# Modulation groups moved beside projections and into routing in a two-network kernel, with early column-half statistics

## The reference, cut to what matters

```python
cs = jax.nn.silu(c)
for l in range(DEPTH):                                   # first network, DEPTH = 2
    mod = (cs @ ada_w[l] + ada_b[l])[:, None, :]         # ada_w[l] is 1024 x 6144
    sh1, sc1, g1, sh2, sc2, g2 = jnp.split(mod, 6, axis=-1)
    h = rms_norm(x, norm1_g[l]) * (1.0 + sc1) + sh1
    ...                                                  # y: even mixer for l = 0, odd mixer for l = 1
    x = x + g1 * y
    h = rms_norm(x, norm2_g[l]) * (1.0 + sc2) + sh2
    x = x + g2 * hier_moe(h, ...)                        # 16 experts of 256 hidden columns, routed
return rms_norm(x, final_g)
...
mod = (c_act @ w_mod[l] + b_mod[l])[:, None, :]          # second network
h = layer_norm(x) * (1.0 + sc1) + sh1
y = hybrid_mixer(...)
x = layer_norm(DEEPNORM_ALPHA * x + (1.0 + gt1) * y, ln1_g[l], ln1_b[l])
h = layer_norm(x) * (1.0 + sc2) + sh2
y = hierarchical_moe(h, ...)                             # 16 experts of 512 hidden columns
x = layer_norm(DEEPNORM_ALPHA * x + (1.0 + gt2) * y, ln2_g[l], ln2_b[l])
```

## Time and profile before

| | us |
|---|---|
| median of 3 runs | 1359.21 |
| lowest, highest | 1359.13, 1361.91 |
| the profiled execution | 1359.62 |
| its span, first to last instruction | 1357.9 |

### The profile page before, as it was taken

The page is one execution under the profiler, slowest core; times in us unless marked ns, Lnnn a source line. Parts: engine busy times, 40 slices in busy tenths (PEclk is TensorE's granted clock), DMA queues, the critical chain, the costliest instruction groups (busy, mean ns, idle before and its releaser), DMA issues.

```text
span 1357.9 us, 17790 instructions
## 1 busy us (share of the span) xinstructions
PE 1232.0 (91%) x7440; PEld 649.5 (48%) x7440; DVE 444.3 (33%) x1148; ACT 267.6 (20%) x621; POOL 115.8 (9%) x202
## 2 busy tenths in 40 slices
PE   4999987999799899799999999899999599999895
PEld 4445743435445665344448845555545343333332
DVE  1102643113203574421153642431132731201124
ACT  0102511122101354212112122002320311020010
POOL 1010010000011000100001000000000222222221
PEclk9899997999999799989999999999999799999998
DMA  9956964999983565469999533383326579999993
GB/s 355 369 177 205 368 202 141 348 373 387 384 291 124 205 233 184 139 211 348 380 386 387 210 124 124 124 300 136 114 101 216 218 253 362 382 387 387 386 385 122
DMA packets 222955, 357.43 MB, mean 263 GB/s; under 512 B 15845, under 2 KB 86038, under 8 KB 222870
## 3 DMA queue, kind: packets, MB, share of 16 engines
q1 hardware_dynamic: 209056, 352.33, 73.6%
q10 hardware_dynamic: 13814, 3.87, 1.3%
HBM read 355.14 MB, written 1.05 MB: 262 GB/s over the span
## 4 chain that ended last, share of the span: by engine, by line
PE 82%; DVE 7%; DMA 4%; ACT 3%; issue 2%; SPq 1%; POOL 0%; DVEq 0%; ACTq 0%
PE bank L2117 20%; PE bank L2318 8%; PE bank L2524 8%; PE bank L2367 4%; PE bank L2810 4%; PE bank L2210 4%; PE bank L2135 4%; DMA ring<-in_w_down 3%; PE bank L2859 3%; PE bank L2293 3%; PE bank L2596 2%; PE bank L2387 2%; PE bank L2202 2%; PE bank L2227 1%; PE bank L2475 1%
## 5 line engine op out<-in xcount | busy, mean ns | idle before, releaser
L2117 PE MATMUL bank<-ring,hT 128*128 128x512 f32 x416 | 183.8, 601 | 3.3 <-ACT hT L895 2.4
L2117 PEld LDWEIGHTS bank<-ring,hT 128*128 128x128 f32 x416 | 79.2, 193 | 99.4 <-issue 98.6
L2524 PE MATMUL bank<-ring,A 128*64 128x512 f32 x512 | 116.5, 601 | 1.8 <-DVE pb L1722 1.8
L2318 PE MATMUL bank<-ring,A 128*64 128x512 f32 x512 | 117.2, 603 | 0.0
L2135 PE MATMUL bank<-ring,cact 128*32 128x128 f32 x2304 | 82.1, 297 | 18.0 <-issue 10.4
L2117 PE MATMUL bank<-ring,OT 128*128 128x512 f32 x224 | 97.2, 593 | 1.3 <-ACT OT L1212 0.8
L751 POOL TENSOR_TENSOR rstd<-rstd,nhalf 128x1 f32<-128x1 f32 x20 | 17.2, 859 | 810.2 <-DVE rstd L1281 810.2
L2135 PEld LDWEIGHTS bank<-ring,cact 128*32 128x32 f32 x2304 | 68.3, 119 | 33.4 <-issue 25.8
L2524 PEld LDWEIGHTS bank<-ring,A 128*64 128x64 f32 x512 | 35.1, 138 | 72.2 <-issue 70.7
L2117 PEld LDWEIGHTS bank<-ring,OT 128*128 128x128 f32 x224 | 42.2, 190 | 53.5 <-issue 52.5
L2318 PEld LDWEIGHTS bank<-ring,A 128*64 128x64 f32 x512 | 34.5, 138 | 66.6 <-issue 66.6
(11 more groups left out here) (470 smaller groups left out, 1663.5 us busy)
## 6 DMA issues: line engine op xcount, KB each, us to landing
ring<-in_ada_w SPq DMA_DIRECT2D x24, 2048.0 KB, 10.1
ring<-in_moe_w_gate SPq DMA_DIRECT2D x32, 1024.0 KB, 8.0
ring<-in_moe_w_up SPq DMA_DIRECT2D x32, 1024.0 KB, 10.6
ring<-in_moe_w_down SPq DMA_DIRECT2D x16, 2048.0 KB, 19.7
ring<-in_w_gate SPq DMA_DIRECT2D x16, 2048.0 KB, 11.6
ring<-in_w_up SPq DMA_DIRECT2D x16, 2048.0 KB, 11.0
ring<-in_w_down SPq DMA_DIRECT2D x16, 2048.0 KB, 20.1
ring<-in_w_in SPq DMA_DIRECT2D x13, 2048.0 KB, 19.6
```

The source lines that it names most:

```text
L2117: ins = mm(B[2 * (m % 2) + tt][:], lhs[:, c, tt * P:(tt + 1) * P], w[:, c, :], start=c == 0, stop=c == C - 1)
L2318: ins = mm(B[r][64 * b:64 * (b + 1), :], wide_h[c][:, slot:slot + 64], w[:, 2 * r + b, :], start=c == 0, stop=c == C - 1)
L2524: ins = mm(B[r][64 * b:64 * (b + 1), :], wide_h[c][:, slot:slot + 64], w[:, 2 * r + b, :], start=c == 0, stop=c == C - 1)
```

## The change

It has four parts.

1. **Order of loads.** `PHASES` interleaves the tiles of `mod_b` with those of `evin` and the tiles of `mod_c` with those of `odin`. `mod_h2` and `mod_h4` move from behind their MoE to the place ahead of it.
2. **Summed by DVE.** For groups 1, 2, 4 and 5 DVE multiplies the eight chunks of a tile by their entries of `cact` and sums them into one 128x512 tile (`mod_sum`, eight instructions, each waiting for the one before). PE adds its 128 rows with four matmuls against ones (`mod_summed_tile`), behind a tile of the projection. The turns come behind tile 3 and at the end. The attentions hold no modulation any more and wait for it ahead of their first scores.
3. **Routing.** In MoE 0 and 1 PE computes the four tiles of groups 3 and 6 in the routing, three between the router and the places and one behind them; the turn stands behind the first gather, DVE's columns ahead of its gathers.
4. **Statistics and halves.** `added` takes the statistics of each column half when it has been added, and the overflow flag is loaded earlier. In MoE 2 the column halves run outside and the experts' halves inside, summed in the bank, so that x is added to twice instead of four times; the last norm's centred product runs ahead of the wait for its power.

The diff, cut to its core:

```diff
-PHASES = [("mod_a", 4), ("evin", 6), ("mod_b", 8), ("evout", 2), ("moe0", 24), ("mod_h2", 4),
-          ("odin", 5), ("cmp", 2), ("mod_c", 8), ("odout", 2), ("moe1", 24), ("mod_h4", 4),
+EVIN = [("evin", 0), ("mod_b", 0), ("evin", 1), ("mod_b", 1), ("mod_b", 2), ("evin", 2), ("mod_b", 3), ("evin", 3),
+        ("mod_b", 4), ("mod_b", 5), ("evin", 4), ("mod_b", 6), ("mod_b", 7), ("evin", 5)]
+ODIN = [("odin", 0), ("mod_c", 0), ("odin", 1), ("mod_c", 1), ("mod_c", 2), ("odin", 2), ("mod_c", 3), ("mod_c", 4),
+        ("odin", 3), ("mod_c", 5), ("mod_c", 6), ("odin", 4), ("mod_c", 7)]
+PHASES = [("mod_a", 4), EVIN, ("evout", 2), ("mod_h2", 4), ("moe0", 24),
+          ODIN, ("cmp", 2), ("odout", 2), ("mod_h4", 4), ("moe1", 24),
           ("xbc", 4), ("z", 2), ("qkv", 3), ("mod_gated", 4), ("ssdo", 2), ("gates", 4), ("atto", 1),
...
+SUMMED = {1: 0, 2: 4, 4: 8, 5: 12}
...
+        def mod_sum(G, k):
+
+            n, order = mod_tile_of(G, k), SUMMED[G] + k
+            acc = tmp[:, order % 2, :]
+            w = ring[n % NSLOT][:].rearrange("p (c n) -> p c n", n=512)
+            dve.wait_ge(landed[n % NSLOT], LANDED[n])
+            if order >= 2:
+                tile_ready(dve, mod_tile_of(*SUM_TILES[order - 2]))
+            step(v.tensor_scalar(acc, w[:, 0, :], cact[:, 0:1], None, ALU.mult))
+            for c in range(1, C):
+                ins = v.scalar_tensor_tensor(acc, w[:, c, :], cact[:, c:c + 1], acc, ALU.mult, ALU.add)
+                if c < C - 1:
+                    step(ins)
+            ins.then_inc(s["mod_summed"], 1)
...
-                for step in mod_chunk_steps(name, t):
-                    mod_tile(*step)
...
+        def mod_summed_tile(G, k):
+
+            if k == 0:
+                pe.wait_ge(s["mod_raw_out"], G)
+            pe.wait_ge(s["mod_summed"], SUMMED[G] + k + 1)
+            acc = tmp[:, (SUMMED[G] + k) % 2, :]
+            for q in range(4):
+                ins = mm(B[MOD_RAW_BANK[G]][32 * q:32 * (q + 1), k * P:(k + 1) * P], tri_one[:, P:P + 32],
+                         acc[:, q * P:(q + 1) * P], start=True, stop=True)
+            ins.then_inc(tile_used, 1)
...
+        def evin_mod(j):
+
+            if j == 3:
+                mod_turn(1)
+            for G, k in (((1, 0),), ((1, 1), (1, 2)), ((1, 3),), ((2, 0), (2, 1)), ((2, 2), (2, 3)), ())[j]:
+                mod_summed_tile(G, k)
+
+        project("evin", 6, hT, turned="h0", between=qk_group, after=evin_mod)
+        mod_turn(2)
         stage_transposed(pe, "qk0")
+        pe.wait_ge(s["mod_ready"], 3)
...
+            for G, k in (((4, 0),), ((4, 1), (4, 2)), ((4, 3), (5, 0)), ((5, 1), (5, 2)), ((5, 3),))[j]:
+                mod_sum(G, k)
...
+                    dve.wait_ge(s["wide_added"], past("wide_added", i) + 2 * j + tt + 1)
+                    step(v.bn_stats(stats[:, tt, j, :], xs))
+            mod_columns(MOE[name]["mod"])
...
+            G = MOE[name]["mod"]
             router(i, MOE[name]["hname"])
+            for k in range(3):
+                mod_tile(G, k)
             places(i)
+            mod_tile(G, 3)
             gather(0, 0)
+            mod_turn(G)
...
-        mod_group(3)
...
-            for half in range(2):
-                for j in range(2):
+            for j in range(2):
+                for half in range(2):
...
+        powers = [norm_begin(x, tt, LN_EPS, True, ()) for tt in range(TT)]
+        dve.wait_ge(s["rows_param"], 16 * 5)
+        for tt in range(TT):
+            step(v.scalar_tensor_tensor(x[:, tt, :], x[:, tt, :], mv[:, tt, 0:1], rowp[:, 0, :],
+                                        ALU.subtract, ALU.mult))
         for tt in range(TT):
             dve.wait_ge(s["pow_done"], powers[tt])
-            gain(tt, 5, True).then_inc(s["result"], 1)
+            v.scalar_tensor_tensor(x[:, tt, :], x[:, tt, :], rstd[:, tt:tt + 1], rowp[:, 1, :],
+                                   ALU.mult, ALU.add).then_inc(s["result"], 1)
```

More of the change, by code:

```diff
@@ L580, in columns, with mixed @@
                      w.rearrange("(c p) n -> p c n", p=P)[:, :, col0 + 512 * j:col0 + 512 * (j + 1)])
+        def mixed(phase, sources):
+            for name, j in phase:
+                w, col0 = sources[name]
+                n = TILE_NO[name, j]
+                load(n, n % NSLOT, kview(n % NSLOT),
+                     w.rearrange("(c p) n -> p c n", p=P)[:, :, col0 + 512 * j:col0 + 512 * (j + 1)])
         def moe_small(name, wg, wu, wd):
@@ L2104, in bank_pair_free, with project @@
                 proj_evacuated(pe, m - 2)
-        def project(name, tiles, lhs, first=0, turned=None, between=None):
+        def project(name, tiles, lhs, first=0, turned=None, between=None, after=None):
             for j in range(first, tiles):
@@ L2124, in project, with mod_tile @@
                         between(g)
-        def mod_tile(G, k, chunks=range(C)):
-            if k == 0 and chunks[0] == 0 and G:
+                if after is not None:
+                    after(j)
+        def mod_tile(G, k):
+            if k == 0 and G:
                 pe.wait_ge(s["mod_raw_out"], G)
@@ L2132, in mod_tile @@
             c0 = C if G >= 6 else 0
-            for c in chunks:
+            for c in range(C):
                 for q in range(4):
@@ L2732, in qkv_group, with odin_mod @@
             transposes("qkv1", from_tokens(pb), [g])
-        project("odin", 5, hT, turned="h2", between=qkv_group)
+        def odin_mod(j):
+            if j == 3:
+                mod_turn(4)
+            for G, k in (((4, 0),), ((4, 1), (4, 2)), ((4, 3), (5, 0)), ((5, 1), (5, 2)), ((5, 3),))[j]:
+                mod_summed_tile(G, k)
+        project("odin", 5, hT, turned="h2", between=qkv_group, after=odin_mod)
         m = PROJ["odin"] + 5
```

160 lines of the change are left out of this document (76 added, 84 removed).

## The result

The changed kernel takes **1394.61 us** (median, 1394.27 to 1395.01), beside 1359.24 us for the kernel before on the same chip: 1.025 of it, 95% interval 1.0235 to 1.0266. The direction is the one forecast. The size is not: +35.4 us where I had +14, and 1394.6 lies outside 1360 to 1380. Its profiled execution has a span of 1393.1 us, 35.2 more than before, and a mean granted clock of 0.944 instead of 0.965.

A forecast was written before the change was run, and what follows sets the result against it. PE, 82% of the chain, was taken to bound the kernel, in the small MoEs together with DMA's weights. Terms 3.5+0+9.2-3.3+7-2.2 = 14.2 gave 1373.8 against the profiled time, 1373.4 against the median: forecast 1373, range 1360 to 1380.

The forecast's parts named there:

- Attention 0 and 1: Both attentions: shorter with the modulation taken out, by 1.0 us in attention 0 and 3.3 us in attention 1.
- The argument about DVE's chain: Attention 0: DVE's chain of 2.4 us stands as before, so an item takes 4.19 us instead of 4.35.
- Rival D: Both attentions lose their clock without modulation, about 4 us each, 8 in both: 1381; chance 0.10.
- Odd projection: Odd projection: 4.0 us for eight summed tiles, turns and switches, and 5.3 of PE wait for DVE's copy: +9.2.
- B: Odd projection: no PE wait, which takes sums of 3.5 us: 1368; chance 0.12.
- C: Odd projection: sums and ropes hold each other, the wait growing by a rope's 2.3 us: 1376; chance 0.12.
- Even projection: Even projection: 3.4 us for small matmuls, a turn and switches, and 1.0 at the end before attention 0.
- MoE 0 and 1: Small MoEs: weight tile t18 lands 6.4 and 7.6 us late, ends 5.9 and 7.0 to 8.7 later.
- Rival A: Small MoEs: a weight queue that never drains recovers 8.4 us at 5.4 a tile: 1360; chance 0.16.
- The tails: Behind MoE 0 8.5 us instead of 17.6, behind MoE 1 15.3 instead of 19.4, plus cold clock of 3.3 and 3.5.
- MoE 0 and its tail, 0: Routing and MoE 0: later end, shorter tail and a cold restart together net 0, range -3.5 to +2.
- Last norm: MoE 2 and last norm: early statistics and the centred product before the power save 2.2 us, range -3 to -1.5.

The follow-up runs named there:

- e5: The changed kernel with idle products, 16 matmuls in each of 8 items of attention 0 and 4, 4, 8 in each three of attention 1; 1396.13 us.
- e1: The changed kernel with idle products in both attentions, in the places and number of the removed modulation matmuls; 1382.55 us, ratio 1.0159.
- e6: The changed kernel with DVE's copy of finished transposed groups ahead of that tile's sums in both projections; 1386.78 us, ratio 1.0204.
- e2: The kernel before with groups 1, 2, 4, 5 summed by DVE beside the projections, and MoE 2's early statistics and flag left in; 1395.28 us.
- e10: The kernel before, unchanged, profiled a second time; span 1357.7 us, time 1359.43 us.
- e3: The kernel before with groups 3 and 6 loaded ahead of the MoE and computed in the routing, MoE 2's early statistics and flag left in; 1367.72 us.
- e4: The kernel before with early statistics, earlier overflow flag and centred product ahead of the power, MoE 2's old order kept; 1357.59 us, ratio 0.9985.
- e8: e7 with idle products on PE, 80 matmuls behind MoE 0 and 176 behind MoE 1; 1363.21 us, ratio 1.0012.
- e7: The changed kernel with only groups 1 and 4 summed, 2, 3, 5, 6 computed in the attentions, MoE 2's old order; 1349.23 us, ratio 0.9907.
- e11: e4 with MoE 2's down tiles in the changed kernel's order, column half outside, expert half inside; 1357.42 us, ratio 0.9972.

## Why the forecast missed, by its own steps

**Attention 0 and 1: the step that failed.** The forecast credited -1.0 and -3.3 for modulation taken out, and kept the clock. The stages came out at +4.1 (with +1.0 behind attention 0) and +6.6: 16 us of the 21 by which the span exceeds my sum. The argument about DVE's chain was right, and e5 shows its -0.9 where the clock stays. What it missed is that the removed products were the ones that kept PE occupied while DVE scaled the scores. e1 shows this: -12 us by idle products alone. Its size in attention 1 is less sure than its cause, since the same gaps gave +3.2 in e6 and +8.1 in e2. Rival D had named the mechanism at a chance of 0.10 and with half its price. It charged a single restart of about 4 us to each attention and forgot that the gains go with it. The clock is not lost once, it is low through long parts of both attentions (0.78 and 0.80). A bound was in reach: all of PE's work at half speed. The page "TensorE: Matmul & The Clock Gate" of the Trainium skill (Part 1, A second HAM failure mode) says that short idle times between groups of matmuls, frequent enough, make the clock go back and forth, and I had not weighed it. Attention 0's timeline, with 1.07 to 2.54 us idle in each item and transposes of 1.51 and 0.85 us, agrees.

**Odd projection: right in mechanism, 2.6 short.** The 5.3 of wait was 4.99, and e6 removes it. Missing were the 1.0 of low clock behind the wait and the 0.7 for ACT. A link of a sum took 752 ns in the median and 787 on average (I had 780): group "L1321", 112 of them, 88.1 us.

```profile
L1321 DVE SCALAR_TENSOR_TENSOR tmp<-ring,cact,tmp 128x512 f32<-128x512 f32 x112 | 88.1, 787 | 4.0
409.80 0.96 POOL L729 TENSOR_TENSOR Pm<-pb,cosd 128x256 f32<-128x256 f32 x1 [12.13 <-DVE pb L515]
```

**Rivals B and C.** B falls with the wait. C is there in small: the rope's first step took 0.96 us beside a sum instead of 0.72, and the seven links 6.31 us instead of 5.47. Of the 4.99 us that is 0.84, not the 2.3 of C. The two engines did not keep each other out throughout: from 409.80 on the four steps of the rope took 3.8 us for what had taken 2.3, while the sum lost 0.84, so for a part of that time both went on.

**Even projection.** +4.1 to the first scores of attention 0, where 3.4+1.0 stood, and +3.0 in e2. That fits, but it proves little: the kernel before itself reached these scores at 126.0 in one profile and at 122.9 in the other (e10).

**MoE 0 and 1.** The lag was right in time and place: t2 at 215.0 as worked out, t18 7.7 late instead of 6.4, the stage +7.4 instead of +5.9, and e3 shows it alone. Rival A's mechanism exists and is small: between t6 and t18 the lag shrank from 249.1-230.8-9.2 = 9.1 to 7.7, at 364 GB/s, where A needed 387. In MoE 1 the 10.1 holds about 2 us of low clock in the routing, for which I had provided 1.7.

**The tails.** I had -5.8 and -0.6 and measured -9.1 and -2.6. The transposes did restart at the low level (3.57 us instead of 1.91), but the measured 8.5 holds this restart, where my 8.5 was worked out without it. That the two numbers agree is luck: the rest of the tail was 1.7 shorter than I had it. With this, "MoE 0 and its tail, 0" was -1.7. My account of the old tail was wrong too: the modulation products were not held back behind the statistics (e4, e8). The early statistics count only once those products are gone: the tail is -6.5 in e3 without them and -9.1 in the changed kernel and e7.

**Second network and MoE 2.** I had 0 for both and the profile shows +1.9 and +2.9. The first lies within what the same kernel shows twice (e10). Of the second, e10 shows 0.7 as spread, and 1.3 to 2.6 come with the earlier statistics (e4, e11); which of their instructions costs it wasn't tried.

**Last norm.** -3.0 against -2.2. e2 and e3 give -2.6 and -2.7 by the statistics and the flag alone, so the centred product adds some 0.4. The wait of the earlier trace rows is gone.

```profile
1384.86 2.59 DVE L2080 SCALAR_TENSOR_TENSOR x<-x,mv,A 128x1024 f32<-128x1024 f32 x2
1387.49 2.48 DVE L2084 SCALAR_TENSOR_TENSOR x<-x,rstd,A 128x1024 f32<-128x1024 f32 x2
```

**Left open:** why the clock stays up in attention 0 with half the idle products and not in attention 1; why attention 1 with empty gaps takes 79.7 us in e6 and 84.7 in e2; whether the loading of instructions sets the waits behind the MoEs, which no run tried; compression, -3.4 in e3 and -2.9 in e2, where e10 has -1.7 without any change; the 0.4 and 0.7 us of e6.

## What to carry to other kernels

Work that fills an engine's waits is not free to remove. Before products are moved out of a stage in which TensorE waits for another engine, price that stage with all its matmuls at the low clock, beside the gain; idle products in their place show within one run which of the two it is.

An instruction put in a row on a busy helper engine delays the short copies behind it: long sums belong behind the copy that the next matmuls need. And a stretch where the main engine has nothing to do is only free if the loads of the work put there have free slots; here the routing was idle and its six slots were not.

## What the chip showed that I had not expected

- The attentions take 37.2 and 76.5 us with PE's waits filled, 41.3 and 83.1 with them empty (granted clock 0.78 and 0.80; 41.1 and 84.7 in e2, 41.8 and 79.7 in e6), and 36.3 and 89.0 with them half filled (1.00 and 0.77). More work on PE made attention 0 shorter by 5.0 us and attention 1 longer by 5.9.
- Behind MoE 0 and 1 short matmuls run in pieces of at most 128 records, with 0.3 to 4.9 us between them in which PE waits for nothing that the profile names. Each time PE went on 2.4 to 2.7 us after the start of a 16 KB packet of instructions.
- Two profiles of one kernel with spans of 1357.9 and 1357.7 differ by 3.6 us in one stage and by 3.0 the other way in another.
